# Depthwise convolution of a two-layer block: two of eight channel tiles moved to GpSimd, the other six tiles' taps spread three to a unit

## What is computed

```python
def conformer_conv_group(a, gate, w_dw, b_dw, ln_g, ln_b):
    u = a * jax.nn.sigmoid(gate)
    u = depthwise_conv(u, w_dw, taps=31, padding=(15, 15)) + b_dw   # 1024 channels, each its own 31 taps
    return jax.nn.silu(layer_norm(u, ln_g, ln_b))                   # over the 1024 channels of a token

def second_block(x, ...):
    h = rms_norm(x, pre_mix_g)
    a, gate, q, k, v = split(h @ w_in)                 # five times 1024 columns
    yc = conformer_conv_group(a, gate, ...)
    ya = neighbourhood_attention_group(q, k, v, rpb)   # 16 heads of 64
    x = x + rms_norm(concat([yc, ya]) @ w_out, post_mix_g)
    h = rms_norm(x, pre_mlp_g)
    return x + rms_norm(square(relu(h @ w_up)) @ w_down, post_mlp_g)
```

## Time and profile before

| what | value |
|---|---|
| median of three runs | 2845.52 us (2835.41 to 2852.19) |
| the profiled execution, by the device's time | 2841.27 us |
| its span in the trace | 2839.3 us |
| PE busy | 2723.7 us (96%) |
| VectorE busy | 2033.5 us (72%) |
| ScalarE busy | 1359.1 us (48%) |
| GpSimd busy | 207.0 us (7%) |
| granted TensorE clock, mean | 0.989 |
| stage `w_in2` | about 1697 to 1973 us |
| the 240 taps | 1725.7 to 1929.8 us |

### The profile page before, as it was taken

One profiled execution on the slowest core, in us unless ns is written; L12 is line 12 of the kernel. 1 busy time (PEld: TensorE's weight loads), 2 busy tenths in 40 slices (PEclk: granted clock), 3 DMA queues, 4 the chain that ended last, 5 costly groups with the idle time before them and its releaser, 6 DMA issues.

```text
span 2839.3 us, 43991 instructions
## 1 busy us (share of the span) xinstructions
PE 2723.7 (96%) x17404; PEld 2453.9 (86%) x17404; DVE 2033.5 (72%) x2989; ACT 1359.1 (48%) x2169; POOL 207.0 (7%) x180
## 2 busy tenths in 40 slices
PE   6988899999999999999999999999999999999997
PEld 6888888998899788888888889998888888888886
DVE  7898787777796886555555679996567566565665
ACT  4445753433444544444444554466554444444454
POOL 0231000000002000000000180111110000000001
PEclk9999999999999999999999999999999999999999
DMA  9864355566787686555555554544445555555553
GB/s 391 315 234 134 104 179 192 195 213 203 255 304 254 224 301 217 189 189 190 189 188 191 186 173 163 180 166 138 157 134 178 191 187 191 186 190 189 186 192 126
DMA packets 158461, 565.37 MB, mean 199 GB/s; under 512 B 17584, under 2 KB 21936, under 8 KB 158256
## 3 DMA queue, kind: packets, MB, share of 16 engines
q1 hardware_dynamic: 158256, 562.56, 58.4%
HBM read 560.39 MB, written 2.10 MB: 198 GB/s over the span
## 4 chain that ended last, share of the span: by engine, by line
PE 84%; DVE 10%; ACT 3%; issue 2%; DMA 1%; SPq 0%; POOL 0%; DVEq 0%; ACTq 0%; POOLq 0%
PE BK L351 20%; PE BK L349 20%; PE BK L352 10%; PE BK L348 10%; PE BK L354 6%; PE BK L356 5%; PE BK L355 5%; DVE LO L659 3%; PE BK L436 2%; ACT HI L519 1%; DVE ADA L655 1%; DVE B L878 1%; DVE B L709 1%; PE BK L361 1%; DVE TV L760 1%
## 5 line engine op out<-in xcount | busy, mean ns | idle before, releaser
L519 ACT ACTIVATE HI<-RAW 128x1024 fp32r<-128x1024 f32 x825 | 875.0, 1061 | 1229.8 <-PE BK L349 846.8
L659 DVE TENSOR_TENSOR LO<-RAW,HI 128x1024 fp32r<-128x1024 f32 x825 | 1017.0, 1233 | 376.8 <-ACT HI L519 374.4
L351 PE MATMUL BK<-H,HI 128*128 128x512 f32 x2528 | 1011.2, 402 | 8.9 <-DVE LO L659 8.5
L349 PE MATMUL BK<-H,HI 128*128 128x512 f32 x2496 | 985.7, 396 | 0.0
L352 PE MATMUL BK<-H,LO 128*128 128x256 f32 x2528 | 703.0, 278 | 0.0
L348 PE MATMUL BK<-H,LO 128*128 128x256 f32 x2496 | 698.4, 280 | 0.4 <-DVE H L705 0.2
L354 PE MATMUL BK<-H,HI 128*128 128x256 f32 x1840 | 547.8, 298 | 35.2 <-DVE B L709 16.8
L348 PEld LDWEIGHTS BK<-H,LO 128*128 128x128 f32 x2496 | 469.8, 188 | 111.5 <-DVE H L705 2.0
L352 PEld LDWEIGHTS BK<-H,LO 128*128 128x128 f32 x2528 | 477.1, 189 | 100.1 <-issue 0.7
L355 PE MATMUL BK<-H,HI 128*128 128x256 f32 x1840 | 525.8, 286 | 0.0
L356 PE MATMUL BK<-H,LO 128*128 128x256 f32 x1840 | 525.5, 286 | 0.0
(11 more groups left out here) (248 smaller groups left out, 1878.8 us busy)
## 6 DMA issues: line engine op xcount, KB each, us to landing
RAW<-wst_dram SPq DMA_DIRECT2D x825, 512.0 KB, 3.3
RAW<-wada_dram SPq DMA_DIRECT2D x155, 512.0 KB, 4.5
EARLY<-wada_dram SPq DMA_DIRECT2D x37, 512.0 KB, 8.9
EARLY<-wst_dram SPq DMA_DIRECT2D x33, 512.0 KB, 7.7
X<-xT_dram SPq DMA_DIRECT2D x8, 512.0 KB, 9.2
B<-bias_dram SPq DMA_DIRECT2D x32, 128.0 KB, 3.3
out_dram<-X SPq DMA_DIRECT2D x3, 512.0 KB, 2.7
CN<-consts_dram SPq DMA_DIRECT2D x1, 900.0 KB, 9.7
```

The lines of the kernel that those rows point to most:

```text
L349: e.matmul(bk[:, :], hh, H[:, k, :], start=False, stop=last, skip_group_check=True).then_inc(S["tile"], 1)
L351: e.matmul(bk[:, :], hh, H[:, k, :], start=first, stop=False, skip_group_check=True)
L519: e.activation(HI[:, u % NHL, :], raw_at(slot), ACT.Copy).then_inc(S["hi"], 1)
L659: e.tensor_tensor(LO[:, u % NHL, :], raw_at(slot), HI[:, u % NHL, :].bitcast(f32), sub).then_inc(S["lo"], 1)
```

## The change

Channel tiles 0 and 1 (`POOLED = 2`) get their taps on GpSimd. A tap is two instructions there: a product of `UP` with the tap's weight into a scratch tile `CT_`, and an addition of `CT_` to `CA[j]`. The new generator `conv_pool` issues one tap every six weight tiles (`POOL_TAP = 6`), from the time that `u_tok[0]` is set. The other six tiles stay on VectorE; `conv_gen` starts with the pair (2, 3), and its counter now counts single taps, with `CONV_STEP = 3`: three VectorE taps per advance in place of four. `conv_norm` now waits for all eight tiles' last taps.

```diff
+POOLED = 2
+POOL_TAP = 6
...
+        CT_ = (B1[:, 17, :], B1[:, 18, :])
...
+            def conv_tap_g(j, i, before, at):
+                q.wait_ge(before)
+                o = COLS["w_dw"][0] + 31 * j
+                e.tensor_scalar(CT_[i % 2], UP[:, j, i:i + 256], CO[:, o + i:o + i + 1], None, mult).then_inc(S["cv_g"], 1)
+                q.wait_ge(("cv_g", at + 1))
+                e.tensor_tensor(CA[j], CA[j], CT_[i % 2], add).then_inc(S["cv_g"], 1)
...
+            def conv_pool():
+                for j in range(POOLED):
+                    while u_tok[j] is None:
+                        yield
+                    k = do("conv_first", "cv_a", j, u_tok[j], b2_free, dw_tok)
+                    for i in range(1, 31):
+                        k = do("conv_tap_g", "cv_g", j, i, [k, b2_free], n=2)
+                        yield
+                    conv_tok[j] = k
+
...
             def conv_gen():
                 n = 0
-                for a in range(0, 8, 2):
+                for a in range(POOLED, 8, 2):
                     while None in u_tok[a:a + 2]:
                         yield
                     k = [do("conv_first", "cv_a", j, u_tok[j], b2_free, dw_tok) for j in (a, a + 1)]
                     for i in range(1, 31):
                         for c in range(2):
                             k[c] = do("conv_tap", "cv_v", a + c, i, k[c])
-                        n += 1
-                        if n % CONV_STEP == 0:
-                            yield
+                            n += 1
+                            if n % CONV_STEP == 0:
+                                yield
                     conv_tok[a:a + 2] = k
                 for _ in xg:
                     yield
-                later(conv_norm(conv_tok[7]), 2)
+                while None in conv_tok:
+                    yield
+                later(conv_norm(conv_tok[:]), 2)
...
-            CONV_STEP = 2
+            CONV_STEP = 3
             cg = conv_gen()
+            later(conv_pool(), 0, POOL_TAP)
```

More of the change, by code:

```diff
@@ L195 @@
            "st_a", "st_v", "st_g", "st_p", "ad_v", "l2_a", "l2_v", "l2_p", "gd_p", "gd_a", "gd_v", "at_p", "at_a",
-           "at_v", "at_g", "cv_a", "cv_v", "cv_p", "spin")
+           "at_v", "at_g", "cv_a", "cv_v", "cv_p", "cv_g", "spin")
 LOADS = tuple(f"raw{i}" for i in range(NRAW + NEARLY)) + tuple(f"bias{i}" for i in range(4)) + ("cols", "consts", "x", "pos", "x2", "out")
@@ L932, in part_add @@
                 e.tensor_tensor(dst, dst, t, add).then_inc(S["ev_g"], 1)
-            walk(dict(part_add=part_add, square_add=square_add, scaled_square=scaled_square, bias_mask=bias_mask))
+            walk(dict(part_add=part_add, conv_tap_g=conv_tap_g, square_add=square_add, scaled_square=scaled_square, bias_mask=bias_mask))
         def walk(mine, log=None):
```

## The result

The kernel after takes 2852.64 us (median of 20 runs), the kernel before 2842.86 us (median of 20 runs): a ratio of 1.0033, 95% interval 1.0024 to 1.0041. That is no change by the bound of 0.5%, though the interval shows a small loss. The forecast was 2861 us, within 2840 to 2877 us.

A forecast was written before the change was run, and what follows sets the result against it. TensorE bounds the kernel, waiting 0.29 us per unit for VectorE beside a and gate; beside attention both are full. Steps of +13.3 us and an end of +2.5 us sum to +15.8 us: 2861 us median, own range 2852 to 2870, whole 2840 to 2877.

The forecast's parts named there:

- rival (a): GpSimd's products are free and only its additions take VectorE time: +5.6 us, 2851 us; chance 0.20.
- step (4): Beside attention: U, VectorE's time for six units, becomes 24.9 us instead of 22.3 us; over 2.3 such periods +6.0 us.
- (1): Convolution starts later, so eight units without VectorE taps run at TensorE's pace: -1.5 us.
- (2): Beside a and gate: 14 units with three taps take 3.70 us instead of 3.17 us: +7.5 us.
- (3): Six units before attention: VectorE's 3.10 us each against TensorE's 2.88 us: +1.3 us.
- end of the convolution: Ends eight units later, so the conv_norm chain falls behind w_in2: +2.5 us, bounds -2 to +15 us.
- a stretch with TensorE under 60% busy: Sign that the forecast is right: expected after L497, itself after the last product of w_in2.
- The low bound of -2 us: At the convolution's end: the attention steps pack as before, without the convolution's VectorE work.
- (b): Relief of VectorE wins and TensorE's 6.4 us of waits go: 2839 us; needs each tap under 0.09 us; chance 0.12.
- (c): After w_in2 the exposed end runs step by step with the clock at 1.2 GHz: +15 us more, 2876 us; chance 0.15.
- (e): The price of GpSimd's taps and VectorE's 23.7 us of relief cancel: 2846 us; chance 0.09.
- (d): GpSimd taps hold VectorE off for whole instructions, 0.74 + 0.93 us: 42 us more, 2903 us; chance 0.02.

The follow-up runs named there:

- experiment 2: Kernel before with all 240 VectorE taps, plus GpSimd's 60 products and 60 additions, the additions written to an unread buffer: stage 422.7 us, ratio 1.0116.
- experiment 8: Kernel before, nothing on GpSimd: convolution started eight units later, stage 388.0 us, ratio 1.000; or three taps a unit beside a and gate, 385.3 us, 0.9988.
- experiment 5: Kernel after with four memsets for each GpSimd product, stage 398.0 us, ratio 1.0031; or three memsets for each addition, 397.3 us, 1.0029.

## Why the prediction was right, and where it was not

The mechanism that the forecast named is the one that the runs show: GpSimd's additions stretch VectorE's two-input instructions, and TensorE waits for LO. That the verdict came out (no change that counts, on the slower side) owes something to luck. The forecast of 2861 us lay 1.3 us beyond the line for slower, and the chances for same and slower were 0.50 and 0.46; the measured 2852.64 us is only just inside the forecast's own range (2852 to 2870) and only 1.6 us from rival (a), 2851 us. Of the 8.4 us between forecast and median 2.4 us are the base (some 2845.2 us in the forecast, 2842.86 us over twenty runs), the rest is the sum: the medians differ by 9.8 us and the stage took +8.9 us where the sum had +15.8 us. The sum has a slip of its own: U in step (4) comes to 24.8 us by its formula, not 24.9, which makes +5.8 us.

Step by step, each from the unit tables (steps (1) and (2) meet at unit 513, at -1.8 us):

| step | forecast | measured |
|---|---|---|
| (1) eight units without taps | -1.5 | -1.8 |
| (2) a and gate, three taps | +7.5 | +7.4 |
| (3) six units before attention | +1.3 | -0.7 |
| (4) beside attention, until 560 | +6.0 | +4.1 |
| end of the convolution | +2.5 | -0.1 |
| sum | +15.8 | +8.9 |

**Steps (1) and (2) held**, and with them their terms. The addition costs 0.48 us and the product 0.15 to 0.22 us, where 0.20 was taken between 0 and 0.23. (The 0.13 us in that upper bound stood on no row. The LO of the earlier trace rows kept its 1.21 us because it came 0.36 us after the product's start, and a product holds VectorE off for its first 0.34 us.) A tap on GpSimd takes 2.50 us ((1801.3 - 1728.8)/29, starts of the first and thirtieth product), where 2.42 was taken. The price of a whole tap at a full VectorE was forecast as 0.61 us and is 0.56 us in experiment 2, over all 60 taps. LO lie 3.81 us apart on the mean between 1759 and 1798 us, where 3.7 us was to be seen.

**Step (3) had the right price and the wrong base.** It took four taps and LO, 2.72 us, to fit under TensorE's 2.88 us in the kernel before. They didn't: relieved of them, the kernel without GpSimd's taps gains 2.0 us in these six units. Against that kernel the kernel after loses 1.4 us there; the forecast had +1.3 against TensorE's own pace. A mean of instruction times under the mean of the unit is not yet cover; that evictions and masks come in bursts is my reading of it, and not shown.

**Step (4) is the same mistake.** Against the kernel without GpSimd's taps the kernel after loses 7.7 us from unit 532 to 560, but that kernel gains 3.6 us on the kernel before between 532 and 536, at the first score steps. Only the first six units beside attention took longer than the 24 to 25 us of the forecast (25.7 us); the following sixes took 21.4 to 23.4 us.

**The end was mis-sized.** I added 36 us of a forced chain and took off 26.5 and 7 us. The 7 us are right (7.4 us between units 560 and 572), the rest is 7.3 us and not 9.5. The same 7.3 us stands in the late start alone (experiment 8), so they are the price of putting sum, squares and scaling behind `w_in2`, whatever GpSimd does. In the kernel after it is paid back in `w_in2` to a tenth, in the late start 6.2 us of it are (units 560 to 572). The sign named for it, a stretch with TensorE under 60% busy, did not come: it is 90% and 80% busy in the two stretches below. The low bound of -2 us was the nearer one. The clock fell to 0.87 on the mean in the earlier trace rows and is 1.00 and 0.94 in the two stretches after; the three stretches aren't the same work, so I draw no more from it than that the exposed end did not cost more clock than the spread one:

```profile
1982.00:2000.00 18.00, 16.20 (x90) 13.41 (x90) 7.28 (x17) 9.19 (x23) 0.73 (x1) 1.00 0.29 95
2000.00:2030.00 30.00, 23.89 (x129) 19.65 (x128) 22.16 (x53) 18.95 (x42) 0.00 (x0) 0.94 0.22 71
```

**A sentence that was false:** "Masks queue behind taps on GpSimd, but are issued three attention steps ahead, over 10 us, against a GpSimd lag of a tap or two." Six units beside attention hold eight taps and four masks in the order (a tap every six of eight steps), which is 8 x 2.50 + 4 x 1.06 = 24.2 us of GpSimd, against 22.0 us of VectorE's work and less once VectorE is relieved. So the lag grows from group to group of masks, and I had counted GpSimd's work only as a price to VectorE, never against its own queue. In the kernel after it hardly shows (2.0 us of VectorE's waits), because the collision made everybody late; once the collision is gone it is most of what is left, and with a slightly slower tap it brings a loss as large as the change's, with 12.4 us in a single wait of TensorE (experiment 5).

**The rivals.** That the products are free (a) is so by themselves and false beside additions, which alone use up the unit's spare time. Its time was the nearest, but by compensation: it gave step (2) +2.9 us where +7.4 us was measured, and its end was 2.6 us and its base 2.4 us too high. That the relief wins (b) fails by its own bound: it wanted a tap under 0.09 us. The exposed end (c) is out: -0.1 us. That price and relief cancel (e) is out as well: 19.1 us of price stand against 10.2 us of relief. That a tap holds VectorE off for 0.74 + 0.93 us (d) is out in its sum, 2903 us, but only the product refutes it. The prediction read 0.48 us as a lock much shorter than the addition; the stretched LO show that VectorE waits until 0.13 us before the addition's end, so for up to 0.61 of its 0.74 us. The product holds it off for 0.34 of its 0.93 us only. The Trainium skill (SBUF — State Buffer, Who interferes with whom) is borne out in the two other things that it says there. A VectorE instruction with at most one SBUF input, outside the engine's 2-port modes, doesn't contend with GpSimd: 174 taps with their sum in PSUM stay between 473 and 490 ns. And one with two contends with a GpSimd instruction that reads SBUF, not with one that only writes: in experiment 5 with four memsets and an addition to each tap, every one of the 180 taps took under 0.5 us or over 0.9 us, as an addition lay beside it or not. Had I weighed its first half when I predicted, it would have named the remedy.

## What to carry to other kernels

Before work goes to GpSimd, write down for each VectorE instruction beside it how many SBUF inputs it has: here a tap with two lost 0.48 us to each 128x256 addition, one with an input in PSUM lost nothing, and moving the running sum there turned 1.0033 into 0.9971. Then look at what already stands in GpSimd's queue: space the new work so that its own pace, not the program's, keeps ahead of whatever another engine waits for; that was another 2.7 us, by one profiled execution of each kernel. And split a change that relieves one engine and loads another into both halves before judging it: here the relief was worth 10.2 us, and spreading the taps alone, with nothing on GpSimd, already gave 3.5 us.

## What the runs showed of the hardware that was not expected

- The collision is a lock, and its length depends on the GpSimd instruction: VectorE goes on 0.13 us before the recorded end of an addition (18 LO of the kernel after), 0.34 us after the start of a product of 0.93 us (2 LO), and loses nothing to a memset of 0.31 us. What an LO loses is what is left of that time when it comes, up to 0.55 us; a tap loses 0.48 us beside an addition of 0.74 us and 0.13 to 0.22 us beside a product.
- It is the price of the second SBUF input alone: with the sum in PSUM the tap's median is 479 ns, with all in SBUF it is 480 ns, so PSUM costs the tap nothing either.
- It goes both ways: a GpSimd instruction that starts inside an LO waits for the end of that LO (2.03 instead of 0.93 us for a product); beside taps a product takes 0.97 us.
- Two delays on a unit with spare time are not additive: products 0, additions 8.4, both 12.0 us by unit 530.
